# A hybrid attention and state-space layer on one core: the opening stage's normalization written another way, and some steps of three instruction queues moved

## What is computed

```python
def _layer(h, pe, past, ...):
    n = _rmsnorm(h, g_in)                       # x * rsqrt(mean(x*x) + eps) * g_in
    z = n @ w_in                                # 2048 -> 6152: q, k, v, forget gate, gate, u, gate
    q, k, v, fl, ga, u, gs = jnp.split(z, ...)
    att = _fox_attention(...)                   # 8 heads of 128
    ssm = _s5(u, ...)                           # diagonal complex state space, GELU, GLU
    mixed = jnp.concatenate([att * silu(ga), ssm * silu(gs)], axis=-1)
    h = h + mixed @ w_out                       # 2048 -> 2048
    e = _rmsnorm(pe @ w_pe, g_pe)               # 256 -> 2048
    h = h + e * sigmoid(h @ w_pg)               # 2048 -> 2048
    return h, k, v, logf, s_re, s_im
y = _rmsnorm(h, g_final)
```

## Time and profile before

| | us |
|---|---|
| median of 3 runs | 2344.55 (2340.38 to 2346.22) |
| the profiled execution | 2348.45 |
| its span in the trace | 2346.6 |
| TensorE busy | 2167.0 (92% of the span) |
| VectorE busy | 1656.2 (71%) |
| ScalarE busy | 999.1 (43%) |
| GpSimd busy | 307.5 (13%) |

### The profile page before, as it was taken

The page is one execution under the profiler, slowest core; times in us unless marked ns, Lnnn a source line. Parts: engine busy times, 40 slices in busy tenths (PEclk is TensorE's granted clock), DMA queues, the critical chain, the costliest instruction groups (busy, mean ns, idle before and its releaser), DMA issues. The chain is left out here.

```text
span 2346.6 us, 44727 instructions
## 1 busy us (share of the span) xinstructions
PE 2167.0 (92%) x16739; PEld 2107.7 (90%) x16739; DVE 1656.2 (71%) x3053; ACT 999.1 (43%) x1863; POOL 307.5 (13%) x459
## 2 busy tenths in 40 slices
PE   3999999999999999999979988988899998999994
PEld 3999999999999999999958867988899998999994
DVE  6779767767786878787536655758667657658775
ACT  6443333333533333334457645324235324335554
POOL 0021000000101111111144320000101221101000
PEclk7999999999999999999989998999999999999997
DMA  8484444444557787877367735454766677857578
GB/s 249 136 269 119 144 128 138 140 129 145 197 171 226 217 232 219 229 217 207 106 210 237 234 111 218 147 178 175 274 238 228 228 272 253 302 174 253 212 253 326
DMA packets 328006, 477.63 MB, mean 204 GB/s; under 512 B 78912, under 2 KB 250280, under 8 KB 318016
## 3 DMA queue, kind: packets, MB, share of 16 engines
q1 hardware_dynamic: 265072, 290.58, 39.8%
q0 software_dynamic: 36976, 139.52, 17.3%
q10 hardware_dynamic: 25760, 44.87, 5.9%
HBM read 295.99 MB, written 170.22 MB: 199 GB/s over the span
## 5 line engine op out<-in xcount | busy, mean ns | idle before, releaser
L757 PE MATMUL acc<-t_act,w_hi 128*128 128x264 f32 x5376 | 888.1, 287 | 9.2 <-DVE zb L1319 7.3
L757 PEld LDWEIGHTS acc<-t_act,w_hi 128*128 128x128 f32 x5376 | 748.9, 189 | 15.6 <-issue 14.2
L2937 PE MATMUL m_acc<-m_t_act,m_hi 128*128 128x264 f32 x3584 | 597.6, 289 | 38.2 <-DVE m_zb L3227 9.6
L757 PE MATMUL acc<-t_act,w_lo 128*128 128x264 f32 x2688 | 548.5, 286 | 0.0
L2937 PEld LDWEIGHTS m_acc<-m_t_act,m_hi 128*128 128x128 f32 x3584 | 506.2, 192 | 42.6 <-issue 28.3
L757 PEld LDWEIGHTS acc<-t_act,w_lo 128*128 128x128 f32 x2688 | 417.8, 189 | 0.0
L2937 PE MATMUL m_acc<-m_t_act,m_lo 128*128 128x264 f32 x1792 | 369.2, 288 | 0.0
L1312 DVE TENSOR_TENSOR w_lo<-w_raw_f,w_hi 128x512 fp32r<-128x512 f32 x288 | 198.0, 687 | 136.0 <-ACT w_hi L967 135.7
L967 ACT CAST w_hi<-w_raw_f 128x512 fp32r<-128x512 f32 x288 | 177.9, 618 | 268.6 <-PE acc L757 240.1
L2937 PEld LDWEIGHTS m_acc<-m_t_act,m_lo 128*128 128x128 f32 x1792 | 282.1, 192 | 0.0
L2986 ACT CAST m_hi<-m_raw 128x512 fp32r<-128x512 f32 x192 | 118.7, 620 | 166.3 <-PE m_acc L2937 125.4
(11 more groups left out here) (429 smaller groups left out, 3391.6 us busy)
## 6 DMA issues: line engine op xcount, KB each, us to landing
w_raw_f<-in_w_in_dram SPq DMA_DIRECT2D x96, 512.0 KB, 3.9
cT<-zb SPq DMA_DIRECT2D x22, 1056.0 KB, 4.2
zb<-cT POOLq DMA_DIRECT2D x88, 264.0 KB, 6.2
zT<-zb POOLq DMA_DIRECT2D x80, 264.0 KB, 4.0
m_e_res<-eT SPq DMA_DIRECT2D x16, 1056.0 KB, 9.6
m_raw<-in_w_out_dram SPq DMA_DIRECT2D x32, 512.0 KB, 6.2
m_raw<-in_w_pg_dram SPq DMA_DIRECT2D x32, 512.0 KB, 6.1
cT<-m_zb SPq DMA_DIRECT2D x12, 1056.0 KB, 5.1
```

Source lines behind the costliest of these rows:

```text
L757: mm = pe.matmul(out[:, c, 0:QN], w[:, k, :], t_act[:, SIDE[r], x, k, c * QN:(c + 1) * QN], start=(opens and k == 0 and m == 0), stop=(k = ...
L2937: mm = pe.matmul(out[:, c, 0:QN], w[:, k, :], t_act[:, MSIDE[r], x, k, c * QN:(c + 1) * QN], start=(opens and k == 0 and m == 0), stop=(k ...
```

## The change

**Opening of the front stage.** VectorE now multiplies the rows of the tile (first 1024 features) by the row factor before they are turned (`scale_rows`, `x_rows`), TensorE turns both the raw tile (`turn_x`, still needed for `xT`) and the scaled one (`turn_rows`), and `normalize` is two multiplications of four feature blocks each, straight from PSUM, by a broadcast gain. The ones matrix, `x_dg` and the eight products per tile are gone. The row factors along the free dimension, which the second half of the features needs, are made by TensorE ahead of products 3 and 5 of pair 0 (`spread`, ten matmuls) and copied by ScalarE in slots 3 and 5 (`copy_bc`). Both gains are loaded as 16 rows of 128 and turned by TensorE. ScalarE takes a root of a constant before the first tile. One low side stands after the second weight sum, the other after the third low part.

**Mix stage.** SP: the residual inputs of pairs 8 and 9 are loaded in pairs 3 and 5 and not in 2, those of pairs 24 and 25 in pairs 21 and 22 and not in 18. POOL: `store_ride` of c = 2 stands first in its pair, and sides 1 to 3 of the second pass change are reloaded between the h stores of pair 15. TensorE turns the gain ahead of product 4 of pair 2 and waits there for its load. VectorE: `add_parts` of pairs 7 and 23 moves from slot 1 to slot 4 of the next pair, and the four residual additions of pair 15 move from slots 5, 6, 0 and 1 to slots 3 to 6 of pair 16.

```diff
+        x_rows = [nc.alloc_sbuf_tensor_at(f"x_rows{b}", [P, D_MODEL // 2], F32, offset=ring_at + 4 * D_MODEL + b * 2 * D_MODEL)
+                  for b in range(2)]
...
                 if t == 0:
-                    with nc.allow_non_contiguous_dma("per-feature columns of the gain"):
-                        sp.dma_start(g_col[:], d["g_in"][0].rearrange("(k p) -> p k", p=P)).then_inc(g_loaded, 16)
+                    sp.dma_start(rstd_bc[0:KD, 0:P], d["g_in"][0].rearrange("(k p) -> k p", p=P)).then_inc(g_loaded, 16)
...
-            def spread(t):
+            def turn_rows(t):
 
                 rows = TILES[t][1]
-                pe.wait_ge(dg_done, t + 1)
-                if t >= 2:
-                    pe.wait_ge(bc_copied, t - 1)
-                pe.matmul(oth[:, t % 2, 0:rows], ones[0:rows, :], dg[t % 2][0:rows, 0:rows], start=True, stop=True) \
-                    .then_inc(bc_done, 1)
+                pe.wait_ge(rows_scaled, t + 1)
+                for h in range(2):
+                    if t:
+                        pe.wait_ge(n_half, 2 * (t - 1) + h + 1)
+                    for f in range(KQ):
+                        tr = pe.transpose(acc[:, 4 + h, f * P:f * P + rows],
+                                          x_rows[t % 2][0:rows, (h * KQ + f) * P:(h * KQ + f + 1) * P],
+                                          ident[0:rows, 0:rows])
+                    tr.then_inc(rows_turned, 1)
+
+            def spread(bank, tiles):
+
+                pe.wait_ge(rstd_done, max(tiles) + 1)
+                for n, t in enumerate(tiles):
+                    rows = TILES[t][1]
+                    mm = pe.matmul(oth[:, bank, n * rows:(n + 1) * rows], stat[0:rows, t, 2:3].to_broadcast([rows, P]),
+                                   ident[0:rows, 0:rows], start=True, stop=True)
+                mm.then_inc(bc_done, 1)
...
+                    if p == 0 and r == 3:
+                        spread(0, (0, 1, 2, 3))
+                        spread(1, (5, 6, 7, 8))
+                    if p == 0 and r == 5:
+                        pe.wait_ge(bc_copied, 1)
+                        spread(0, (4, 9))
...
             act.wait_ge(consts, 1)
+            nc.scalar.activation(stat[:, 0, 3:4], eps[:], ACT.Sqrt)
             for t in range(10):
                 square(t)
                 root(t)
-                copy_x(t)
+                if t:
+                    copy_x(t - 1)
...
-            def spread(t):
+            def scale_rows(t):
...
-                TS(dg[t % 2][0:rows, 0:rows], ident[0:rows, 0:rows], stat[0:rows, t, 2:3], None, ALU.mult) \
-                    .then_inc(dg_done, 1)
...
+                TS(x_rows[t % 2][0:rows], x_in[t][0:rows, 0:D_MODEL // 2], stat[0:rows, t, 2:3], None, ALU.mult) \
+                    .then_inc(rows_scaled, 1)
...
-                for f in range(8):
-                    s = STT(n_raw[:, f // 4, f % 4, tok:tok + rows], x_t[t][:, f, 0:rows], g_col[:, f:f + 1],
-                            rstd_bc[:, tok:tok + rows], ALU.mult, ALU.mult)
-                s.then_inc(n_done, 1)
+                for h in range(2):
+                    dve.wait_ge(rows_turned, 2 * t + h + 1)
+                    TT_(n_raw[:, h, :, tok:tok + rows], acc[:, 4 + h].rearrange("p (f t) -> p f t", f=KQ)[:, :, 0:rows],
+                        g_col[:, h * KQ:(h + 1) * KQ].unsqueeze(2).to_broadcast([P, KQ, rows]), ALU.mult) \
+                        .then_inc(n_half, 1)
...
                 if p == 2:
                     sp.wait_ge(t_ready, 7)
-                    load_residual(NPM)
-                    load_residual(NPM + 1)
-                    with nc.allow_non_contiguous_dma("per-feature columns of the gain"):
-                        sp.dma_start(g_pe[:], d["g_pe"][0].rearrange("(k p) -> p k", p=P)).then_inc(gains_loaded, 16)
+                    sp.dma_start(x_part[0][0:KD, 0:P], d["g_pe"][0].rearrange("(k p) -> k p", p=P)) \
+                        .then_inc(gains_loaded, 16)
+                if p in (3, 5):
+                    load_residual(NPM + (p - 3) // 2)
...
-                if p == 2 * NPM + 2:
+                if p in (2 * NPM + 5, 2 * NPM + 6):
                     put_landed(2 * NPM - 1)
-                    load_residual(GATE)
-                    load_residual(GATE + 1)
+                    load_residual(p + 3)
...
             for p in range(NPM, 2 * NPM):
                 r = p - FIRST_RIDE[2]
+                if 1 <= r <= NRIDE:
+                    store_ride(2, r - 1)
                 if p == 2 * NPM - 1:
                     reload_side(2, 0)
...
                     if p > NPM:
                         store_h(p - 1, n)
-                if 1 <= r <= NRIDE:
-                    store_ride(2, r - 1)
+                    if p == 2 * NPM - 1 and n > 0:
+                        reload_side(2, n)
...
-            for s in range(1, 7):
+            for s in range(4, 7):
                 reload_side(2, s)
...
+                    if p == 2 and r == 4:
+                        pe.wait_ge(gains_loaded, 16)
+                        pe.transpose(oth[:, 0, 0:KD], x_part[0][0:KD, 0:P], ident[0:KD, 0:KD]).then_inc(gains_turned, 1)
...
-                    if p and mix_opens(p - 1) and j == 1:
+                    if p and mix_opens(p - 1) and j == (1 if mix_opens(p) else 4):
                         add_parts(p - 1)
...
-                    if NPM <= p < 2 * NPM and j >= 5:
+                    if NPM <= p < 2 * NPM - 1 and j >= 5:
                         residual(p, j - 5)
-                    if NPM < p <= 2 * NPM and j < 2:
+                    if NPM < p < 2 * NPM and j < 2:
                         residual(p - 1, j + 2)
+                    if p == 2 * NPM and j >= 3:
+                        residual(p - 1, j - 3)
```

89 lines of the change are left out of this document (51 added, 38 removed).

## The result

The changed kernel takes 2318.48 us (median of four runs, 2316.01 to 2325.11) against 2345.07 for the kernel before; the ratio is 0.9895, with a 95% interval of 0.987 to 0.9919. That is 26.6 us less, where 34 were forecast. Its profiled execution took 2318.57 us with a span of 2316.8, against 2348.45 and 2346.6, so the two traces are 29.8 apart.

A forecast was written before the change was run, and what follows sets the result against it. TensorE, busy 92% of the span, was taken as the bound, with gains only from its idle time and slow clock. Terms summed to 34.1 us: 2348.45 to 2314.4 profiled, less 3.9 gives 2310.5; 8-in-10 range 2301 to 2326.

The forecast's parts named there:

- worked-out case: The whole kernel: all terms sum to 34.1 us, median 2310.5, own range 2303 to 2318; chance 0.55.
- Opening: Front stage start: first product at 53.8, 9.1 us earlier, less 2.3 for spreads; 7.0 gained (5 to 10.5).
- The table loads: ScalarE's opening: two loads of 1.28 us move ahead of the first tile's landing, 2.56 earlier.
- the rival with the first product at full clock: Opening and pair 2: first product at 2.4 GHz and gain's row in time, 5.7 us more gain, 2305; chance 0.12.
- Pair 2: Mix: the 12.1 us lost to the late `eT` block go, a 2.2 wait for the gain's row comes; 8.9 gained.
- Pairs 3 and 5: Mix: a residual block ahead of `scale_e`'s block costs at most 5.3 us, nearly 4 to spare; -0.3 (-3 to 0).
- First pass change: Pair 8: with `add_parts` moved, the gap falls from 3.94 to 2.0 us; 3.0 gained (1 to 5).
- Pairs 13 to 16: Second pass change: earlier ride stores end the ride waits, 3.0 of 17.3 us lost stays; 14.3 gained (6 to 16.5).
- the side reloads stay the bound: Second pass change: four sides still must come before pair 16, some 9 of the 14.3 us stay lost; 2319.5, chance 0.20.
- The rival of the late part loads: `load_part`, now behind the ride's four stores, makes `seed_x` late and the kernel slower than before; 2351 us, chance 0.02.
- Pair 19: Mix: residual blocks moved to pairs 21 and 22 end VectorE's 6.35 us ride wait; 3.7 gained (1.5 to 3.7).
- Pair 24: Third pass change: three gaps merge into one of about 3.7 us before product 6, half clock behind; -2.5 (-4 to 0).

The follow-up runs named there:

- table_first: The kernel before plus only ScalarE's root of a constant ahead of the first tile; first product starts at 60.80 us, against 62.87.
- open_only: The kernel before with only the changed kernel's opening of the front stage, nothing of the mix stage; 2336.36 us against 2343.43, ratio 0.997.
- gain_r5: The changed kernel with the gain turned ahead of product 5 of pair 2, not product 4; pair 2 takes 20.90 us, against 24.69.
- res_late: The changed kernel with the residual blocks of pairs 3 and 5 issued behind the `eT` block, not ahead; pair 4 takes 20.55 us, against 23.0.
- h14_late: The changed kernel with three of pair 14's four h stores issued behind the side reloads; pairs 15 and 16 take 47.3 us, against 49.8.
- ride_back2: The changed kernel with GpSimd's queue as before in pairs 12 to 15, the moved residual additions kept; 2330.87 us, ratio 0.9942.
- half_sides: The changed kernel with half of each side block reloaded at the second pass change, casts and subtractions whole; pairs 15 and 16 take 46.55 us.
- res24_back: The changed kernel with the residual blocks of pairs 24 and 25 loaded in pair 18 again; pair 19 takes 21.70 us, against 20.4.
- ride_back: First execution of the same kernel as ride_back2, GpSimd's queue as before in pairs 12 to 15; 4443.83 us.

## Why the prediction was right, and where it was off

*The bound and the measure.* TensorE's idle time was the right thing to count: the undisturbed pair is 20.44 to 20.56 in every kernel, and the gains are where the gaps were. The result, 2318.48, is inside the range of 8 in 10 (2301 to 2326), but 0.5 above the range that the worked-out case was given for itself (2303 to 2318).

*Opening: right in its parts; on the average two misses cancel.* First product 53.28 for 53.8, tile 4.84 for 4.85, scaling 0.75 for 0.70, spreads 1.95 for 2.3. The table loads gave 2.07 and not 2.56 (table_first), since the second tile's landing took the place of the rest. VectorE still reached the second half 5.5 earlier (31.27 for 36.77) where 4.4 were counted, and took 0.6 more from there: some 1.6 beyond the loads and the wait of 1.81 came from the rest of the new opening, and no run splits them. What was held at "a little", the lead of the low sides and the clock of the first product, was 1.6: ScalarE's first copy of an accumulator stands 5.76 behind the first product (59.04) and not 7.34 (70.21). Of it the clock is about 0.7; the rival with the first product at full clock did not come true, since the first 4.1 us of it still ran at 1.2 GHz. At the same copy in front pair 23 the gain is 9.6 for 7.0, and the changed kernel's trace gains another 1.5 up to mix. But this trace is the luckiest of eleven: the average gain at the end of the front stage is 7.3 (see open_only), so the forecast left out both a larger gain in the opening and a loss of some 3 at front pairs 28 and 29. That the average meets the 7.0 is luck.

*The rules of the clock and of the table load.* TensorE in the changed kernel's opening:

```profile
5.95 1.94 PE L701 MATMUL acc<-ident,x_in 128*128 128x128 f32 x8 [5.95 <-DMA x_in<-in_x_prompt_dram]
...
9.89 1.04 PE L713 MATMUL acc<-ident,x_rows 128*128 128x128 f32 x8
```

Eight transposes take 1.94 at 5.95 and 1.04 at 9.89, and TensorE had done nothing but transposes until then, so the clock rose behind transposes alone (granted clock 1.00 from 10 to 14, 0.50 from 30 to 34, where they run again). The rule that transposes don't count for the clock (the Trainium skill, "TensorE: Matmul & The Clock Gate", "Part 4: PE-mode transpose") does not agree with this trace. On the drain of 1.4 us that the Trainium skill ("ScalarE: Activation LUTs", "What ACT_TABLE_LOAD costs") adds to a load: in table_first the two loads that were taken off the path brought 2.07, less than their own 2.56, so no run here shows a drain beside them.

*Pair 2: right.* 8.0 for 8.9. The new wait was 2.19 for 2.2. What came on top of it was 1.9 for 1.0, in this execution: 1.6 of slow clock and 0.3 that stays without the wait (gain_r5).

*Pairs 3 and 5: undersized.* The step that failed is the comparison of "at most 5.3" with "nearly 4 to spare": it took the `eT` block as on time but for what the change puts ahead of it. In pair 3 the block is 1.56 late by itself (res_late), the residual block adds 4.2, inside the 5.3, which makes 5.78, and less the spare time of 3.6 (VectorE came at 1668.0, `c12` was wanted at 1674.9 and takes 3.3 with the scaling ahead of it) this is TensorE's gap of 2.22. In three other executions the slow clock came on top and the pair lost 3.9 to 4.0, outside the range of -3 to 0. Pair 5 lost nothing.

*First pass change: right* in size (3.0). The gap is 2.49 and not 2.0. The clock behind it fell in eight of the ten kernels with this edit; in the two others (res_late, h14_late) a gap of 1.1 ahead of product 6 follows instead, and the pair takes 23.2 to 23.8 in all of them.

*Pairs 13 to 16: the term that was mis-sized,* 8.6 for 14.3. Its mechanism, the order of GpSimd's queue, is shown (ride_back2). The step that failed is "what stays: ... I leave 3.0". 8.7 stay, and 5.4 of them have nothing to do with the queue: with low sides of 2.35 in a row VectorE needs 3.47 per product (half_sides). The clause that slots 3 to 6 of pair 16 are "where VectorE has room" failed with it: VectorE is busy 6.00 of 6.00 there, and the moved additions lengthen the wait for `c22` from 0.9 to 2.0, behind which the clock fell in this execution (1.4). The numbers were in hand, since the prediction names "five low sides of 2.35 beside VectorE's usual work", but it did not set their sum per product against 2.94. The rival "the side reloads stay the bound" gave 2319.5, nearer to the result than the worked-out case, for a reason that covers only about 1.8 of the 8.7. The rival of the late part loads did not come true: pairs 13 and 14 take 20.55 each.

*Pair 19: right in size by luck.* 3.85 for 3.7 in this pair of traces, but the loads explain 0.4 to 1.1 in three other executions (res24_back, open_only, table_first); the trace of before was an unfavourable one.

*Pair 24: right.* -2.7 for -2.5, with the gap (3.39 for 3.7) and the slow clock. Over eight kernels it is -1.4, since the clock does not always fall and the fall does not always cost the same.

*The sum.* 2318.5 lies 8.0 above the forecast. Of that 4.3 are in the traces, 29.8 for 34.1: pairs 13 to 16, pair 2 and pair 3 were too high by 5.7, 0.9 and 2.1, the opening and what follows it in the front stage too low by 4.1, of which 3.1 is the luck of this trace against the average of eleven. The rest lies between traces and medians: the profiled execution before was taken as 3.9 above its median, that after is at its own.

## What to carry to other kernels

Where a stage is about to become free of a long wait, add up the work of the second busiest engine per step of the first and compare the two periods; that, and not an allowance, is what stays. A wait for a small transfer should stand as late in the waiting engine's program as its reader allows: one product later cost nothing and gave 3.8 us. Merging small gaps into a large one on TensorE is no saving even where the idle sum is equal: the clock may fall behind either, but behind the last gap nothing takes the loss up. A gain at the start of a long stage should be read again at its end, over several executions.

## What the runs showed of the hardware

The clock's fall behind one and the same gap is not fixed. Behind 3.38 to 3.40 us without a matmul it fell in seven of eight executions, at a cost of 1.3 to 2.6 us; behind 2.15 to 2.19 us in six of eight, at 1.5 to 1.6; behind 2.01 to 2.04 us, ahead of product 6 of pair 16, in three of eight, at 1.4 to 1.5. One trace of such a place gives one draw. The time of the next four matmuls (0.72 to 1.25 us) does not tell whether it fell: in ride_back2 they took 0.76 behind the gap of 2.15 and the pair still took 24.63.

The row of 8 KB that SP issued at 1634.33, 0.4 behind a weight block of 512 KB, landed at 1640.6, 6.3 later; VectorE got the weight block at 1640.35. In this place the small transfer behind a large one landed no sooner than the large one, and TensorE waited 2.15 to 2.19 for it in all eight executions.

In the execution of ride_back that took 4443.83 us the large matmuls took 0.48 us on the average, against 0.29 in the changed kernel, while the busy time of VectorE stayed as it was (1669.8 us against 1650.3). Four matmuls in a row took 1.17 us there (at 1000.26) and take 1.08 at granted clock 0.50 in the kernel before (at 1791.24), which is what 1.2 GHz throughout would look like. The trace cannot confirm it: it holds no record of the granted clock at all, and the 1.00 that is shown for it stands for that. What slowed TensorE there is not in the trace.
